# A fused attention and PEER block on one NeuronCore: both kv heads in one sliding unit, the key scores reloaded at other tiles, and other row counts in the searches and the tail

## The chip, the core and the metric

The kernel runs on one core of one Trainium2 chip. The metric is the device time of one execution in microseconds. TensorE is the matrix engine, VectorE the vector engine, ScalarE does activations and copies, GpSimd does some subtractions and issues gathers, SyncE issues most DMA transfers. In views of the profile they are PE (PEld for weight loads), DVE, ACT, POOL and SP.

## The reference

512 tokens of 1024 numbers go through a sliding-window attention with 8 heads on 2 kv heads, a latent attention with 8 heads, an output projection, and then a PEER layer: each token picks 16 of 16384 experts for each of 8 heads by two top-16 searches over 128 sub-keys and one over their sums, and adds up the picked experts.

```python
scores = jnp.einsum('bcqkgd,bcskd->bckgqs', qc, kb)            # sliding window: k = kv head, g = head in its group
scores = scores - slopes[None, None, :, :, None, None] * dist[:, :, None, None]
...
o = jnp.einsum('bckgqs,bcskd->bcqkgd', p / denom, vb)
x = x + gate1 * (jnp.concatenate([out_a, out_b], axis=-1) @ w_out)
...
s_top, i_top = lax.top_k(s, K)                                  # s: scores against the 2 x 128 sub-keys of a head
best, bi = lax.top_k(cand, K)                                   # cand: sums of the two lists of 16
a = jax.nn.gelu(jnp.einsum('tkd,td->tk', u_table[eb], xb), approximate=False)
y = jnp.einsum('tk,tkd->td', gb * a, v_table[eb])
```

## The kernel before

**Attention.** Work comes in units of one block of 128 queries. There are 16 sliding units (4 blocks, each with 2 kv heads and 2 pairs of query heads) and 32 latent units (4 blocks by 8 heads). For a sliding unit TensorE makes two score products in `scores` (L1028): both with the 64 rows of one kv head as contraction, so both use the same half of the array's rows, and both write one bank of PSUM, `u % 3`. VectorE adds the distance bias and takes the maximum (`bias_and_max`), ScalarE takes the exponentials, VectorE scales, TensorE transposes (L1041), ScalarE copies, TensorE multiplies by the values (L1058), VectorE copies out. In a step u TensorE issues `scores(u + 2)`, `transposes(u)`, `values(u - 1)`. `scores(u)` waits until the exponentials of unit u - 3 are done.

**The dense part of PEER.** 352 of the 512 tokens are computed against all 16384 experts: 128 tiles of the u table in a dot phase (`dot`, L1178 to L1180, 24 matmuls a tile), then 128 tiles of the v table in a mix phase (`mix`, L1229 to L1231). Each tile is loaded by SyncE into one of 3 buffers `raw`, rounded by ScalarE into `hi` (`high`), and its remainder is put into `lo` by GpSimd (`low_u`, L554), in the mix phase by VectorE (`low_v`). SyncE issues the load of tile m once the `lo` of tile m - 3 is done.

**The sparse part.** The other 160 tokens are computed from gathered expert rows. 128 of them have 128 row slots, the last 32 are spread over 4 partitions each and have 32 further slots: 160 u rows and 160 v rows in all, each a gather of 128 x 1024 numbers (512 KB), issued by GpSimd (`gather`, L567) into one of 7 buffers, four of which (`row_res`) lie where `res` was. Gather g waits until VectorE has used row g - 7. VectorE takes the dot product of a u row with the tokens (`row_dot`, L1549) and adds up a weighted v row (`row_sum`, L1684). A table `row_step` tells GpSimd after which tile each gather is issued, and the loops on VectorE have the matching counts.

**The searches.** `search(p)` for the four blocks of tokens runs on VectorE: `search(0)` first, and `search(1)` to `search(3)` during tiles 11 to 27, 44 to 60 and 77 to 93. Each reads the key scores from one tile `s`; for p of 1 to 3 SyncE reloads it from `keys` (L493, 1 MB) after it has waited for `s_free`, which VectorE raises when the first half of `search(p - 1)` is through with `s`. This load is at the tile `search_at[p - 1] + 10`, that is 10, 21 and 54. In a search VectorE makes a row dot at some of 15 pauses, `FILL[p]` in all. After each search come tiles in which TensorE also builds gates from one-hot matrices (28 to 43, 61 to 76, 94 to 105; L1189), with 2 or 3 row dots a tile. `turn_slots` (L1196) at the first of them waits for the end of the search.

**The tail.** In the tiles from 106 on (`tail_at`) there are no searches. VectorE does the 32 further row dots, planned at 3 a tile. At every sixth of them it also makes the `lo` of one tile (`own_low`: tiles 109, 111, 113, 115, 117, 119; L1694), so that GpSimd has a `lo` at every second tile and issues 6 gathers between. After the gelu of the dot products VectorE adds up 4 v rows (`EARLY`) ahead of the mix phase and the other 156 in it, 5 in every 4 tiles. After the last row sum SyncE reloads `res` from `x1` (L516, 2 MB), and VectorE makes the output from it (L1722).

## Time and profile before

| | us |
|---|---|
| median of 3 runs | 1495.96 |
| lowest and highest | 1495.47, 1498.05 |
| the profiled execution | 1498.4 |
| its span | 1496.6 |
| TensorE busy | 1419.4 (95%) |
| VectorE busy | 1207.9 (81%) |
| GpSimd busy | 744.9 (50%) |
| ScalarE busy | 708.8 (47%) |

Mean granted clock of TensorE: 0.967 of full speed. The span goes, in order of time, through the first projections (to 157 us), the attention (157 to 272), the output projection and the queries (to 384), the dot phase (384 to 1001), the mix phase (1001 to 1486) and the output. A busy TensorE is one that has a matmul under way, and does not tell at which clock. So the views to read are the waits of TensorE, the windows with the granted clock, and for each wait the order of time on the engine that it waits for.

### The profile page before, as it was taken

How to read it: one execution, taken by the hardware profiler on the slowest of the kernel's cores; microseconds unless marked ns; L12 is line 12 of the kernel's file. 1: busy time of each engine (PE TensorE's matmuls, PEld its weight loads, DVE VectorE, ACT ScalarE, POOL GpSimd, SP SyncE). 2: the span in 40 equal slices, each digit the busy share in tenths (PEclk: the TensorE clock that was granted, in tenths of full speed). 3: DMA queues.
4: the chain of work that ended last, by engine and by line, in shares of the span. 5: the costliest groups of instructions: out<-in, count | busy, mean ns of one | idle time of the engine just before them, and what ended most of it. 6: DMA issues, size and time to landing. Idle time of an engine off the chain costs nothing.

```text
span 1496.6 us, 23445 instructions
## 1 busy us (share of the span) xinstructions
PE 1419.4 (95%) x8415; PEld 1297.8 (87%) x8415; DVE 1207.9 (81%) x2637; ACT 708.8 (47%) x1315; POOL 744.9 (50%) x472
## 2 busy tenths in 40 slices
PE   3998999989998899999999998899999999999999
PEld 1464666768898899989999998899999999999998
DVE  4757567774878888958897876569999999999997
ACT  1245556331543588448854883243443434443342
POOL 2001000120577788768777876744555655565540
PEclk9999569999999999999999999899999999999999
DMA  9920100353678899999999999989999999999996
GB/s 330 328 84 1 56 1 1 119 205 127 211 248 286 314 340 338 360 389 319 328 348 402 335 325 359 404 263 373 397 388 389 382 401 392 398 390 389 394 386 229
DMA packets 158083, 438.79 MB, mean 293 GB/s; under 512 B 16592, under 2 KB 50704, under 8 KB 156816
## 3 DMA queue, kind: packets, MB, share of 16 engines
q1 hardware_dynamic: 91488, 244.55, 45.3%
q0 software_dynamic: 46080, 167.79, 29.4%
q10 hardware_dynamic: 20400, 24.95, 4.7%
q8 instruction: 67, 1.10, 0.3%
q14 instruction: 48, 0.39, 0.1%
HBM read 390.02 MB, written 47.22 MB: 292 GB/s over the span
## 4 chain that ended last, share of the span: by engine, by line
PE 83%; DMA 6%; DVE 4%; POOL 3%; ACT 2%; issue 1%; SPq 0%; ACTq 0%; DVEq 0%
PE ps L1230 11%; PE ps L1231 11%; PE ps L1229 11%; PE ps L1178 8%; PE ps L1180 8%; PE ps L1179 8%; PE ps L1189 5%; PE ps L947 4%; PE ps L1058 2%; POOL lo L554 2%; DMA raw<-in_u_tiles 2%; DMA row_res<-in_u_rows,E 2%; PE ps L1028 2%; PE ps L1041 2%; DMA ring<-in_w_ada 2%; PE ps L1031 1%
## 5 line engine op out<-in xcount | busy, mean ns | idle before, releaser
L804 ACT ACTIVATE hi<-raw 128x1024 fp32r<-128x1024 f32 x256 | 271.2, 1060 | 316.1 <-PE ps L1231 199.9
L554 POOL TENSOR_TENSOR lo<-raw,hi 128x1024 fp32r<-128x1024 f32 x122 | 293.3, 2408 | 156.0 <-ACT hi L804 155.3
L1178 PE MATMUL ps<-h2hi,hi 128*128 128x352 f32 x1024 | 339.6, 332 | 22.9 <-DVE lo L1694 11.6
L1180 PE MATMUL ps<-h2hi,lo 128*128 128x352 f32 x1024 | 334.6, 327 | 0.0
L1179 PE MATMUL ps<-h2lo,hi 128*128 128x352 f32 x1024 | 334.0, 326 | 0.0
L1230 PE MATMUL ps<-clo,hi 128*128 128x352 f32 x1008 | 324.2, 322 | 0.0
L1231 PE MATMUL ps<-chi,lo 128*128 128x352 f32 x1008 | 324.2, 322 | 0.0
L1229 PE MATMUL ps<-chi,hi 128*128 128x352 f32 x1008 | 324.1, 322 | 0.0
L567 POOL DMA_INDIRECT row_res<-in_v_tiles,E x91 | 153.0, 1681 | 134.9 <-DVE y_tok L1684 101.3
L1178 PEld LDWEIGHTS ps<-h2hi,hi 128*128 128x128 f32 x1024 | 196.8, 192 | 26.1 <-POOL lo L554 13.1
L1179 PEld LDWEIGHTS ps<-h2lo,hi 128*128 128x128 f32 x1024 | 195.8, 191 | 0.0
L1180 PEld LDWEIGHTS ps<-h2hi,lo 128*128 128x128 f32 x1024 | 195.4, 191 | 0.0
L1231 PEld LDWEIGHTS ps<-chi,lo 128*128 128x128 f32 x1008 | 189.3, 188 | 0.0
L1229 PEld LDWEIGHTS ps<-chi,hi 128*128 128x128 f32 x1008 | 189.3, 188 | 0.0
L1230 PEld LDWEIGHTS ps<-clo,hi 128*128 128x128 f32 x1008 | 189.3, 188 | 0.0
L1671 DVE TENSOR_TENSOR lo<-raw,hi 128x1024 fp32r<-128x1024 f32 x128 | 156.4, 1222 | 20.9 <-ACT hi L804 18.3
L567 POOL DMA_INDIRECT rows<-in_v_tiles,E x69 | 114.3, 1657 | 85.3 <-DVE y_tok L1684 67.7
L826 ACT ACTIVATE act_out<-ps 128x352 f32<-128x352 f32 x128 | 59.4, 464 | 140.6 <-PE ps L1180 127.7
L1549 DVE SCALAR_TENSOR_TENSOR row_res<-row_res,ps 128x1024 f32<-128x1024 f32 x91 | 108.7, 1216 | 12.0 <-DMA row_res<-in_u_rows,E 11.8
L837 ACT ACTIVATE ohW<-eqI,wS 128x128 f32<-128x128 f32 x352 | 107.4, 391 | 7.3 <-DVE eqI L1604 7.3
L567 POOL DMA_INDIRECT row_res<-in_u_rows,E x91 | 90.2, 991 | 30.8 <-issue 16.1
L1549 DVE SCALAR_TENSOR_TENSOR rows<-rows,ps 128x1024 f32<-128x1024 f32 x69 | 82.7, 1215 | 18.3 <-DMA rows<-in_u_rows,E 18.0
(293 smaller groups left out, 2202.8 us busy)
## 6 DMA issues: line engine op xcount, KB each, us to landing
raw<-in_u_tiles SPq DMA_DIRECT2D x128, 512.0 KB, 5.7
raw<-in_v_tiles SPq DMA_DIRECT2D x128, 512.0 KB, 7.2
gelus<-act_out ACTq DMA_DIRECT2D x128, 176.0 KB, 5.5
act_in<-gelus SPq DMA_DIRECT2D x128, 176.0 KB, 8.8
gates<-stage SPq DMA_DIRECT2D x32, 512.0 KB, 8.7
gate<-gates SPq DMA_DIRECT2D x32, 512.0 KB, 9.1
late<-in_w_ada SPq DMA_DIRECT2D x4, 2048.0 KB, 8.0
qkT<-in_w_ada SPq DMA_DIRECT2D x3, 2048.0 KB, 21.6
```

Of the source, the lines that this page charges most:

```text
L554: nc.gpsimd.tensor_tensor(lo[m % 3][:], raw[m % 3][:], hi[m % 3][:].bitcast(F32), ALU.subtract).then_inc(u_lo, 1)
L567: nc.gpsimd.indirect_dma_start(rows[g % NROWS], None, table, bass.IndirectOffsetOnAxis(ap=at, axis=0)).then_inc(row_in[g % NROWS], 16)
L804: nc.scalar.activation(hi[m % 3][:], raw[m % 3][:], ACT.Copy).then_inc(t_hi, 1)
L837: last = nc.scalar.activation(ohW[half][:, t, :], eqI[:, half, t, :], ACT.Copy, scale=wS[:, col:col + 1])
L1178: nc.tensor.matmul(out, hi[n % 3][:, cols], dense(h2hi, k), start=(k == 0), stop=False)
L1179: nc.tensor.matmul(out, hi[n % 3][:, cols], dense(h2lo, k), start=False, stop=False)
L1180: last = nc.tensor.matmul(out, lo[n % 3][:, cols], dense(h2hi, k), start=False, stop=(k == KD - 1))
L1229: nc.tensor.matmul(out, hi[m % 3][:, cols], chi[n % 4][:], start=(n == 0), stop=False)
L1230: nc.tensor.matmul(out, hi[m % 3][:, cols], clo[n % 4][:], start=False, stop=False)
L1231: last = nc.tensor.matmul(out, lo[m % 3][:, cols], chi[n % 4][:], start=False, stop=False)
L1549: nc.vector.scalar_tensor_tensor(out=row, in0=row, scalar=1.0, in1=x_tok, op0=ALU.mult, op1=ALU.mult, accum_out=aa[:, g:g + 1]).then_inc(r ...
L1671: tt_(lo[m % 3][:], raw[m % 3][:], hi[m % 3][:].bitcast(F32), ALU.subtract).then_inc(v_lo, 1)
```

## The change

Five things are changed.

1. A sliding unit is now one head g of both kv heads. Its two score products take rows 0 to 63 and rows 64 to 127, and write two banks of PSUM, (0, 1) or (2, 7) by turns. `scores(u)` for these waits for the bias of unit u - 2 and no longer for the exponentials; unit 0 also waits for the copy of a third block of queries. The rows of `w_out` are permuted on the host to match. The count and the shapes of all instructions stay.
2. The key scores are reloaded at tiles 6, 31 and 64.
3. The searches have 12, 10 and 10 row dots for 15, 9 and 9.
4. The tail has 2 row dots a tile for 3, GpSimd makes every `lo` of the dot phase, and the gelu of the row dots is at tile 125 (`more_at`), ahead of that tile's own gelu, for after tile 122.
5. No v row is added up ahead of the mix phase: all 160 are in it, still 5 in every 4 tiles, so that the last four come at its last three tiles.

```diff
-        units = [("s", b, kv, j) for b in range(TT) for kv in range(SKV) for j in (0, 2)] + \
+        units = [("s", b, None, g) for b in range(TT) for g in range(SG)] + \
                 [("m", b, h, 0) for b in range(TT) for h in range(MH)]
...
+        def score_bank(u, half):
+            return (0, 1, 2, 7)[2 * (u % 2) + half]
...
-        FILL, PAUSES, EARLY, MORE = {1: 15, 2: 9, 3: 9}, 15, 4, 4
+        FILL, PAUSES, MORE = {1: 12, 2: 10, 3: 10}, 15, 4
...
-        sums_at = [n for n in range(NT) for _ in range(2 if n % MORE == MORE - 1 else 1)][:SU - EARLY]
-        more_at = tail_at + 5 + (SU - SLOTS) // 3
-        row_step = row_step[:SLOTS] + [tail_at + 2 + j // 3 for j in range(SU - SLOTS)] + \
-            [more_at + 1 + j // 3 for j in range(EARLY)] + [NT + n for n in sums_at]
+        sums_at = [n for n in range(NT) for _ in range(2 if n % MORE == MORE - 1 else 1)][:SU]
+        more_at = tail_at + 3 + (SU - SLOTS) // 2
+        row_step = row_step[:SLOTS] + [tail_at + 2 + j // 2 for j in range(SU - SLOTS)] + [NT + n for n in sums_at]
...
-        own_low = [tail_at + 3 + 2 * j for j in range((SU - SLOTS) // 6 + 1)]
...
-                    if m == search_at[p - 1] + 10:
+                    if m == (6 if p == 1 else build_at[p - 1] + 3):
                         sp.wait_ge(s_free, p)
...
-                if m not in own_low:
-                    low_u(m)
+                low_u(m)
...
+                if n == more_at:
+                    act.wait_ge(row_used, SU)
+                    nc.scalar.activation(cc[:], aa[:], ACT.Gelu).then_inc(aa_gelu, 1)
                 if n >= NT - 3:
                     high_c(n - (NT - 3))
                 gelu(n)
...
-                if n == more_at + 1:
-                    act.wait_ge(row_used, SU)
-                    nc.scalar.activation(cc[:], aa[:], ACT.Gelu).then_inc(aa_gelu, 1)
...
                 if u == 0:
-                    pe.wait_ge(zq_sb, 2)
-                if u >= 3:
+                    pe.wait_ge(zq_sb, 3)
+                if 2 <= u < NSU + 3:
+                    pe.wait_ge(biased, min(u - 1, NSU))
+                if u >= NSU:
                     pe.wait_ge(exp_done, u - 2)
...
-                    rows = slice(sub * SD, (sub + 1) * SD)
-                    for j in range(2):
-                        c0 = j * 256 + (256 - len(tiles) * P)
-                        last = nc.tensor.matmul(ps[:, u % 3, c0:c0 + len(tiles) * P], qTs[rows, j0 + j, q], kcT[rows, 0, keys_],
+                    c0 = 512 - len(tiles) * P
+                    for half in range(2):
+                        rows = slice(half * SD, (half + 1) * SD)
+                        last = nc.tensor.matmul(ps[:, score_bank(u, half), c0:512], qTs[rows, j0, q], kcT[rows, 0, keys_],
                                                 start=True, stop=True)
...
             for g in range(SLOTS, SU):
-                if (g - SLOTS) % 6 == 0:
-                    m = own_low[(g - SLOTS) // 6]
-                    dve.wait_ge(t_hi, m + 1)
-                    tt_(lo[m % 3][:], raw[m % 3][:], hi[m % 3][:].bitcast(F32), ALU.subtract).then_inc(own_lo, 1)
                 row_dot(g)
...
-            for n in range(EARLY):
-                row_sum(n)
```

The diff shows a table entry where whole orders move, so the order of two queues stands here. First SyncE around tile 21. `raw` is a tile's load, `s<-keys` the reload that first waits for `s_free`. Before:

```order
L459 DMA raw_138<-in_u_tiles 128x1024
L493 DMA s<-keys 128x2048
L459 DMA raw_139<-in_u_tiles 128x1024
L459 DMA raw_140<-in_u_tiles 128x1024
L459 DMA raw_138<-in_u_tiles 128x1024
```

and now, at tile 31:

```order
L457 DMA raw_139<-in_u_tiles 128x1024
L491 DMA s<-keys 128x2048
L457 DMA raw_140<-in_u_tiles 128x1024
L457 DMA raw_138<-in_u_tiles 128x1024
L457 DMA raw_139<-in_u_tiles 128x1024
```

The reload stood behind the load of tile 21 and ahead of that of tile 22; it now stands ten tiles later.

Then GpSimd in the tail. `lo` is a tile's low part, `rows` and `row_res` are gathers. Before, around tile 114:

```order
L554 TENSOR_TENSOR lo_144<-raw_138,hi_141 128x1024
L567 DMA rows_149<-in_u_rows,E_133 128x1024
L567 DMA rows_150<-in_u_rows,E_133 128x1024
L567 DMA rows_151<-in_u_rows,E_133 128x1024
L567 DMA row_res_152<-in_u_rows,E_133 128x1024
L567 DMA row_res_153<-in_u_rows,E_133 128x1024
L567 DMA row_res_154<-in_u_rows,E_133 128x1024
L554 TENSOR_TENSOR lo_146<-raw_140,hi_143 128x1024
```

and now:

```order
L552 TENSOR_TENSOR lo_144<-raw_138,hi_141 128x1024
L565 DMA rows_151<-in_u_rows,E_133 128x1024
L565 DMA row_res_152<-in_u_rows,E_133 128x1024
L552 TENSOR_TENSOR lo_145<-raw_139,hi_142 128x1024
L565 DMA row_res_153<-in_u_rows,E_133 128x1024
L565 DMA row_res_154<-in_u_rows,E_133 128x1024
L552 TENSOR_TENSOR lo_146<-raw_140,hi_143 128x1024
```

Two low parts with six gathers between them (the low part of the tile between was on VectorE) have become a low part at every tile with two gathers after it. That pattern runs from tile 110 to 125.

## Rows read from the trace of the kernel before

**Rows 1.** Waits of PE, 384 to 1005 us: waiter, releaser, total us, times, longest.
```profile
PE ps L1178 <- DVE lo L1694: 11.6, 4, 4.6
PE ps L1178 <- POOL lo L554: 11.3, 5, 4.4
PE ps L1196 <- DVE IJW L1598: 7.1, 1, 7.1
```

**Rows 2.** Chain that ended last, in order of time: start, us, what.
```profile
202.53 2.00 PE ps L1028 x4
204.54 1.04 PE ps L1041 x4
205.58 1.06 PE ps L1058 x8
...
374.05 2.07 PE ps L1146 x32
```

**Rows 3.** Windows: stretch, busy us of each engine, PEclk, DMA share, GB/s.
```profile
184.00:192.00 8.00, 8.00 (x33) 5.15 (x32) 4.82 (x16) 3.28 (x10) 0.00 (x0) 0.50 0.00 1
...
770.00:825.00 55.00, 55.00 (x343) 54.84 (x342) 45.87 (x173) 23.47 (x31) 40.83 (x23) 1.00 1.02 389
...
956.00:964.00 8.00, 4.28 (x15) 4.28 (x15) 4.65 (x7) 1.17 (x2) 5.96 (x4) 0.66 1.03 415
```

**Rows 4.** Timeline of a sliding unit: start, us, engine line op [idle before <-releaser].
```profile
188.15 0.75 DVE L1435 SCALAR_TENSOR_TENSOR pb<-distm,ps 128x256 f32<-128x256 f32 x2 [1.63 <-PE ps L1028]
```

**Rows 5.** Timeline, tiles 19 to 22: low part, loads, first matmul of tile 22.
```profile
454.42 2.40 POOL L554 TENSOR_TENSOR lo<-raw,hi 128x1024 fp32r<-128x1024 f32 x1 [0.35 <-ACT hi L804]
...
463.59 0.33 SPq L493 DMA_DIRECT2D s<-keys  x1
463.96 15.86 SPq L459 DMA_DIRECT2D raw<-in_u_tiles  x5
...
476.02 0.66 PE L1178 MATMUL ps<-h2hi,hi 128*128 128x352 f32 x1 [4.37 <-POOL lo L554]
```

**Rows 6.** Timeline of search(1): start, two row dots, an index search, turn_slots after it.
```profile
431.79 3.18 DVE L1529 MAX8 sv<-s 128x8 f32<-128x128 f32 x16
443.21 1.22 DVE L1549 SCALAR_TENSOR_TENSOR rows<-rows,ps 128x1024 f32<-128x1024 f32 x1 [8.24 <-DMA rows<-in_u_rows,E]
...
448.09 0.28 DVE L1532 FIND_INDEX8 six<-sv,s 128x8 uint32<-128x128 f32 x1
...
482.01 1.22 DVE L1549 SCALAR_TENSOR_TENSOR rows<-rows,ps 128x1024 f32<-128x1024 f32 x1 [4.82 <-DMA rows<-in_u_rows,E]
...
508.72 0.90 PE L1196 MATMUL ps<-ident,IJW 128*128 128x128 f32 x3 [7.11 <-DVE IJW L1598]
```

**Rows 7.** Chain in order of time at tile 55, and its first matmul (timeline).
```profile
629.06 13.60 DMA raw<-in_u_tiles
...
646.25 0.43 PE L1178 MATMUL ps<-h2hi,hi 128*128 128x352 f32 x1 [3.19 <-POOL lo L554]
```

**Rows 8.** Timeline: a GpSimd set (low part, second gather), first matmuls of tiles 112, 127.
```profile
879.92 2.40 POOL L554 TENSOR_TENSOR lo<-raw,hi 128x1024 fp32r<-128x1024 f32 x1
...
883.75 0.94 POOL L567 DMA_INDIRECT row_res<-in_u_rows,E  x1 [0.30 <-issue]
...
918.68 0.33 PE L1178 MATMUL ps<-h2hi,hi 128*128 128x352 f32 x1
...
997.29 0.32 PE L1178 MATMUL ps<-h2hi,hi 128*128 128x352 f32 x1
```

**Rows 9.** Timeline of the end: a row sum, reload of res, output.
```profile
1475.01 1.28 DVE L1684 SCALAR_TENSOR_TENSOR y_more<-row_res,cc,y_more 128x1024 f32<-128x1024 f32 x1
...
1479.60 0.33 SPq L516 DMA_DIRECT2D res<-x  x1
...
1487.24 4.05 DVE L1722 SCALAR_TENSOR_TENSOR res<-ps,ada,res 128x512 f32<-128x512 f32 x6 [5.91 <-DMA res<-x]
...
1493.04 0.75 DVE L1722 SCALAR_TENSOR_TENSOR res<-ps,ada,res 128x512 f32<-128x512 f32 x1 [0.55 <-PE ps L1250]
```

More of the change, by code:

```diff
@@ L292, in build @@
         u_lo = sem("u_lo")
-        own_lo = sem("own_lo")
         v_lo = sem("v_lo")
@@ L398, in build @@
         assert len(row_step) >= SLOTS
-        sums_at = [n for n in range(NT) for _ in range(2 if n % MORE == MORE - 1 else 1)][:SU - EARLY]
-        more_at = tail_at + 5 + (SU - SLOTS) // 3
-        row_step = row_step[:SLOTS] + [tail_at + 2 + j // 3 for j in range(SU - SLOTS)] + \
-            [more_at + 1 + j // 3 for j in range(EARLY)] + [NT + n for n in sums_at]
+        sums_at = [n for n in range(NT) for _ in range(2 if n % MORE == MORE - 1 else 1)][:SU]
+        more_at = tail_at + 3 + (SU - SLOTS) // 2
+        row_step = row_step[:SLOTS] + [tail_at + 2 + j // 2 for j in range(SU - SLOTS)] + [NT + n for n in sums_at]
         assert len(row_step) == 2 * SU
-        own_low = [tail_at + 3 + 2 * j for j in range((SU - SLOTS) // 6 + 1)]
-        def low_done(m):
-            mine = sum(o <= m for o in own_low)
-            return (own_lo, mine) if m in own_low else (u_lo, m + 1 - mine)
         x_tok = ps[:, 4:6, :].rearrange("p a c -> p (a c)")
@@ L454, in load_tile @@
                 if 3 <= m < NT + 3:
-                    sp.wait_ge(*low_done(m - 3))
+                    sp.wait_ge(u_lo, m - 2)
                 elif m >= NT + 3:
@@ L1053, in values @@
                     if kind == "s":
-                        v = z[:, kb, Z_V + sub * SD:Z_V + (sub + 1) * SD]
+                        v = z[:, kb, Z_V + half * SD:Z_V + (half + 1) * SD]
                     else:
@@ L1172, in dot @@
             def dot(n):
-                pe.wait_ge(*low_done(n))
+                pe.wait_ge(u_lo, n + 1)
                 pe.wait_ge(gelu_done, n + 1)
@@ L1460, in copy_out @@
                 if kind == "s":
-                    ins = nc.vector.tensor_copy(oT[:, 2 * sub + j0 // 2, cols], ps[:, 3 * (u % 2) + 3, 0:P])
+                    ins = nc.vector.tensor_copy(oT[:, j0, cols], ps[:, 3 * (u % 2) + 3, 0:P])
                 else:
@@ L1715, in _ @@
                     if at == n:
-                        row_sum(EARLY + j)
+                        row_sum(j)
                 if n + 3 < NT:
@@ L1748 @@
         "mla_norms": np.stack([a["mla_q_norm"][0], a["mla_k_norm"][0]], 1),
-        "w_out": a["w_out"][0], "peer_w_query": a["peer_w_query"][0],
+        "w_out": np.concatenate([a["w_out"][0][:SH * SD].reshape(SKV, SG, SD, D).transpose(1, 0, 2, 3).reshape(SH * SD, D),
+                                 a["w_out"][0][SH * SD:]]), "peer_w_query": a["peer_w_query"][0],
         "sub_keys": a["peer_sub_keys"][0].transpose(1, 3, 0, 2).reshape(P, PH, NK),
```

7 lines of the change are left out of this document (4 added, 3 removed).

## The prediction

> **What bounds the kernel now.** I read the waits of TensorE first, then windows for the granted clock, then for each wait the timeline of the engine it waits for. In the dot phase TensorE is the bound wherever it is not stopped: 343 matmuls in 55.0 us, 0.160 us each, so 24 of them, one tile, take 3.85 us [rows 3]. It is stopped by three kinds of waits, 30 us in all: 11.6 for low parts on VectorE, 11.3 for low parts on GpSimd, 7.1 for the end of search(1) [rows 1]. In the sliding units of the attention it is never idle, 8.00 of 8 us, but at half the clock [rows 3], and a unit is the plain sum of its three pieces: 2.00 for scores, 1.04 for transposes, 1.06 for values [rows 2]. VectorE waits 1.63 us a unit for the scores [rows 4]. In the mix phase TensorE is busy without a gap. So what counts is what TensorE does in the units, and when each low part and the end of search(1) come.
>
> **Paired kv heads.** Nothing is added; the two products of a unit change from the same array rows to different ones. The nearest row is that of the key scores, the same form (64 rows in turn from either half, different banks): 16 products of 128 columns in 2.07 us at full clock [rows 2]. The unpaired 256 columns take 1.00 us each at half clock, which is 0.25 for 128 columns at full clock, so 16 would take 4.0: pairs take 0.52 of that. A unit's scores then take 1.04 instead of 2.00. Bounds: no overlap at all, gain 0; complete overlap, gain 1.00. I take 0.96, since the row is of this very form. Twelve units have 256 columns: 12 x 0.96 = 11.5 us. The four with 128 columns lie beside VectorE's work at the start; I count nothing (0 to 1). What is late next: TensorE's unit shrinks from 4.10 to 3.14, VectorE is busy 4.82 of 8 us, 2.47 a unit [rows 3], so TensorE stays the bound, with 0.6 to spare. The new wait for the bias of two units back was met long before, and the wait for a third block of queries holds TensorE only where it turned heads anyway. **-11.5**, between -9.5 and -13.
>
> **The reload at tile 21 and search(1).** The low part of tile 19 is done at 454.42 + 2.40 = 456.8, which frees the load of tile 22. It goes at 463.96, right behind the reload at 463.59, which waited for search(1) to let go of `s` [rows 5]. Seven microseconds late, it makes TensorE wait 4.37 us. At tile 31 search(1) is over and nothing waits. What is late next is search(1) itself: TensorE waits for its end at the first gate tile until 508.72, for 7.11 us [rows 6]. Without the first stall tile 22 starts at 476.02 - 4.37 = 471.65 and tile 28 is reached six tiles later, at 494.75. Does VectorE get there by then? It starts at 431.79 and needs 76.6 us until 508.4. Of this 8.24 and 4.82 are waits for rows [rows 6]. The second came because GpSimd's gather stood behind the late low part; it goes. Of the first, 4.0 us go: with 12 rows the first pause has none, and the 16 index searches after it (444.4 to 448.4 [rows 6]) now stand ahead of the first row. Three row dots of 1.2 us go to later places: 3.5. Together 76.6 - 4.8 - 4.0 - 3.5 = 64.3: the search ends at 496.1, or somewhat before if later rows are waited for less too. That is 0 to 1.3 behind tile 28. TensorE's gain is 508.7 - 495.4 = 13.3, and some 0.7 of slower clock after the stall. **-14**, between -10 and -15. The reload at tile 6 meets `s_free` within 1 us of it, with buffers to spare: 0.
>
> **Searches 2 and 3.** The reload at tile 54 puts 1 MB into a stretch that is full: the load of tile 55 took 13.60 us and TensorE waited 3.19 [rows 7]. Search(3) has the same gates and no reload, and there TensorE is busy 55.0 of 55 us at 389 GB/s [rows 3]. So the 3.2 go. Each search gets one more gather, 0.52 MB, 1.35 us at that rate, somewhere between hidden and paid in full. The reloads at 31 and 64 lie in gate tiles, which last longer for much the same traffic; their 2.7 us of transfer are covered by three `raw` and seven row buffers. **-2.5**, between 0 and -3.5.
>
> **The tail.** Tile 112 starts at 918.68 and tile 127 at 997.29 [rows 8]: 78.6 us for 15 tiles that take 57.8, so 20.8 are lost, to the four waits for VectorE's low parts (which stood behind row dots that waited for gathers), to one of 2.3 us for GpSimd's low part, and to the clock that fell with them, to 0.66 in one stretch [rows 3]. Now GpSimd has every low part and two gathers a tile. One such set takes 884.69 - 879.92 = 4.77 us [rows 8], against 3.85 for TensorE: GpSimd becomes the bound, by 0.92 a tile. It runs from tile 110 to 125, 15 steps, 13.8 us. Its lead takes some of this away: three buffers let it start two tiles, 7.7 us, ahead, less its own 2.40 and ScalarE's rounding; I take 3 (0 to 5). So 11 to 12 are lost where 20.8 were. **-9**, between -2 and -13. Transfers: 0.52 MB for the tile, 1.05 for two rows, 0.18 for gelus are 1.75 MB, 4.2 us at the 415 GB/s that the tail reached [rows 3], below 4.77. The Trainium skill has less ("SBUF — State Buffer", section "A bandwidth-pool intuition that's wrong"): about 358 GB/s between HBM and a core. By that a tile would take 4.9 us, and by an estimate from it the tail would gain 2 us less; the rows with 389 and 415 GB/s speak against it.
> The gelu of the row dots at tile 125 waits for the last row dot, whose gather goes at tile 122; what is queued behind it on ScalarE is that tile's gelu, for which tile 127 waits. I see a microsecond of room and count 0 (0 to 2).
>
> **The end.** Before, the reload of `res` goes at 1479.60, lands at 1487.2, and VectorE has been idle since 1481.33 [rows 9]. The last row sums now come after tile 127's low parts: 1481.3 plus four of 1.28 is 1486.4. The reload takes the same 7.6 us, to 1494.0, and now VectorE's eight output steps of 0.675 (4.05 for six) all lie behind it: 1499.4, where the last ended at 1493.79. **+5.6**, between +5 and +7: the cover for this reload was TensorE's last two tiles, and it is gone.
>
> **Sum.** -11.5 - 14 - 2.5 - 9 + 5.6 = -31.4. The profiled execution took 1498.4 (span 1496.6), 2.4 above the median; the difference is taken from the median: 1495.96 - 31.4 = 1464.6.
>
> **Rivals.**
> A, *the clock comes up in the sliding units*. Row pairs keep more of the array at work. The rows only say that a busy TensorE stays at 0.50 there [rows 3]. At 2.4 GHz its unit would be 1.57 us and VectorE's 2.47, with some 0.1 of handover, would bound: 3.14 - 2.6 = 0.54 less, 12 times, 6.5 us: 1458. The Trainium skill ("TensorE: Matmul & The Clock Gate", Part 1) has activity release the clock; by that alone the stage would have been at full clock before, and the row disagrees. Its Part 4 says that transposes don't count as activity, which would fit. Chance 0.15.
> B, *the tail gives nothing*. GpSimd's sets stretch or loads come late, as in the 415 GB/s stretch, and 20.8 are lost again: 1464.6 + 9 = 1474. Against it: the rate asked for is 367 GB/s at 4.77 us a tile. Chance 0.16.
> C, *the pairs don't overlap*, the change doesn't do what it says: 1464.6 + 11.5 = 1476. Against it the key scores' row. Chance 0.07.
> D, *slower*: TensorE, with a gap in each tile of the tail, is granted half the clock there. A tile would take 7.7 instead of 4.77: 2.9 for 15 tiles, 44 us, 1508. It decides from 11 such tiles on. For it: 0.66 in a stretch with waits [rows 3]. Against: that had a wait of 4.6 us [rows 1], here they are 0.9. Chance 0.04.
>
> **How the numbers follow.** The forecast has 0.58, its own range 1459 to 1472 from the bounds above, not all at one end. The range must take in most of A and B: 1456 to 1476, which leaves out D, half of C and the outer ends of the others. Only D is slower by over 0.2%, and nothing but a mixture of B, C and a worse end lands within 0.2% (about what can be told from no change): faster 0.95, same 0.01, slower 0.04.
>
> **What would show it.** Scores of a unit in about 1.04 in the chain, and the granted clock there; no wait of the reload at its new tiles; `turn_slots` waiting under 2 us and reached near 495 less the attention's gain; no 3 us wait in search(2); low part and two gathers each 4.8 us in the tail, with waits of TensorE under 1 us; the reload of `res` 7 us later against the last tiles, and eight output steps in a row. Wrong it would be if the tail's loads are late, or if search(1) ends several microseconds after tile 27.

## The result, and the profile after

| | before | after |
|---|---|---|
| median, us | 1496.62 (1495.47 to 1498.05, 4 runs) | 1463.50 (1462.56 to 1464.45, 4 runs) |
| profiled execution: time, span, mean granted clock | 1498.4, 1496.6, 0.967 | 1464.15, 1462.3, 0.986 |
| first dot (tile 0) | 384.16 | 364.83 |
| tile 112, tile 127 | 918.68, 997.29 | 886.40, 956.24 |

The changed kernel takes 0.9778 of the time before (95% interval 0.9761 to 0.9795), 33.1 us less. The forecast was 1464.6, with a range of 1456 to 1476. The total is right. Two of its five terms are not: they miss by 7.8 and 5.6 us, in opposite directions.

To see that, the two traces are laid beside each other by the starts of the tiles. Each term of the sum has its edit between two such marks, and the marks of the two kernels can be subtracted. What a stretch takes also depends a little on where it starts: pair_alone below shows 2 to 3 us of that in stretches whose code is unchanged.

| stretch | term | before, us | after, us | difference | predicted |
|---|---|---|---|---|---|
| start to tile 0 | paired heads | 384.16 | 364.83 | -19.3 | -11.5 |
| tile 0 to tile 29 | reload, search(1) | 131.74 | 123.39 | -8.4 | -14 |
| tile 29 to tile 112 | searches 2 and 3 | 402.78 | 398.18 | -4.6 | -2.5 |
| tile 112 to tile 127 | tail | 78.61 | 69.84 | -8.8 | -9 |
| tile 127 to the end of the span | end | 499.31 | 506.06 | +6.8 | +5.6 |
| sum | | | | -34.3 | -31.4 |

**The page of the changed kernel.** TensorE's busy time, the granted clock in 40 slices, and the shares of the chain that ended last by engine:

```profile
PE 1390.9 (95%) x8415; PEld 1274.4 (87%) x8415; DVE 1200.6 (82%) x2631; ACT 710.3 (49%) x1315; POOL 772.1 (53%) x478
...
PEclk9999799999999999999999999999999999999999
...
PE 80%; DVE 7%; POOL 4%; DMA 4%; ACT 2%; issue 1%; SPq 1%; ACTq 0%; DVEq 0%; POOLq 0%
```

The clock row has one low digit, the fifth (146 to 183 us), in which the sliding units begin.

**The waits of TensorE** in the changed kernel, from the first dot to the end (waiter, releaser, total us, times, longest); they answer to [rows 1]:

```profile
PE ps L1177 <- POOL lo L552: 9.6, 14, 1.1
PE ps L1195 <- DVE IJW L1597: 4.4, 1, 4.4
PE ps L1248 <- DVE y_more L1683: 3.2, 1, 3.2
```

Waits for VectorE's low parts are gone, since VectorE has none left. GpSimd's are many and short where they were few and long: the tail has a bound now, and no stalls (the 1.1 is at tile 3; in the tail none is over 0.7). The wait for search(1) fell from 7.1 to 4.4 where 0 to 1.3 was predicted. The last row is new, and belongs to the end.

**The sliding units.** Windows of the changed kernel, TensorE alone (stretch, its length, busy us, PEclk, DMA share, GB/s), and one with all engines (PE, PEld, DVE, ACT, POOL); they answer to the first window of [rows 3]:

```profile
160.00:170.00 10.00, 9.34 (x44) 0.55 0.32 119
172.00:174.00 2.00, 2.00 (x13) 0.50 0.00 0
174.00:176.00 2.00, 2.00 (x18) 0.85 0.00 0
176.00:178.00 2.00, 1.55 (x18) 1.00 0.00 0
...
180.00:188.00 8.00, 6.50 (x60) 3.88 (x56) 7.72 (x28) 5.59 (x17) 0.00 (x0) 1.00 0.01 3
```

In the full units the granted clock is first at the lower of its two levels, as before, and at the higher one, 2.4 GHz, from 176 us on. What the engine did before it rose: from 162 us on it was busy without a gap, with pairs, transposes and values. Before, it was as busy, with single score products, and the clock stayed at 0.50 up to 214. While the clock is at 0.50, the chain that ended last has the score products of a unit (start, us, what; two products, each in two records) as

```profile
164.70 1.16 PE ps L1027 x4
```

where the kernel before has 2.00 [rows 2]. From 176 us on VectorE is the busiest engine (7.72 of 8 us) and TensorE waits for it: one unit follows the other in 2.38 us.

**Search(1).** Its first step on VectorE starts at 412.39, and `turn_slots` gets its result at 479.83. Timeline, [idle before <-releaser], and windows behind this wait, here and (the last line) behind the 7.11 us wait of the kernel before:

```profile
479.83 0.90 PE L1195 MATMUL ps<-ident,IJW 128*128 128x128 f32 x3 [4.38 <-DVE IJW L1597]
...
480.40:485.00 4.60, 4.60 (x18) 4.60 (x17) 4.23 (x8) 2.45 (x8) 3.79 (x4) 0.50 1.03 417
485.00:488.00 3.00, 3.00 (x24) 3.00 (x23) 1.13 (x3) 0.80 (x2) 1.76 (x2) 0.97 1.03 416
...
509.00:514.00 5.00, 5.00 (x26) 5.00 (x26) 4.34 (x8) 2.45 (x8) 4.52 (x4) 0.75 1.03 408
```

The clock is at 0.50 until about 485.2, 5.3 us behind the wait. Before, with the longer wait, it was at 0.50 for only 2.8 us behind it (0.75 in the mean of the 5 us shown).

**The tail.** GpSimd's queue, timeline, as in [rows 8]:

```profile
878.08 2.41 POOL L552 TENSOR_TENSOR lo<-raw,hi 128x1024 fp32r<-128x1024 f32 x1
880.65 0.96 POOL L565 DMA_INDIRECT row_res<-in_u_rows,E  x1 [0.16 <-issue]
881.91 0.94 POOL L565 DMA_INDIRECT row_res<-in_u_rows,E  x1 [0.30 <-issue]
882.87 2.43 POOL L552 TENSOR_TENSOR lo<-raw,hi 128x1024 fp32r<-128x1024 f32 x1
```

One set takes 882.87 - 878.08 = 4.79 us (predicted 4.77), and from tile 114 to 125 each tile takes 4.77 to 4.79.

**The end.** Timelines of SyncE's queue and of VectorE; they answer to [rows 9]:

```profile
1443.27 2.70 DVE L1683 SCALAR_TENSOR_TENSOR y_more<-row_res,cc,y_more 128x1024 f32<-128x1024 f32 x2
...
1445.99 0.33 SPq L514 DMA_DIRECT2D res<-x  x1
...
1454.01 5.36 DVE L1715 SCALAR_TENSOR_TENSOR res<-ps,ada,res 128x512 f32<-128x512 f32 x8 [8.04 <-DMA res<-x]
```

The last row sum ends at 1445.97, the reload goes 0.02 us later, and all eight output steps lie behind its landing, 5.36 us in a row.

### The profile page after: what moved, and what is told of

Same layout as the page of the kernel before. It is cut to its first block, busy times and chain, and to the rows that moved or that the text cites. A ratio compares the mean times of both kernels' runs of the same rounds, so it can differ in the third digit from the quotient of the medians.

```text
span 1462.3 us, 23449 instructions
## 1 busy us (share of the span) xinstructions
PE 1390.9 (95%) x8415; PEld 1274.4 (87%) x8415; DVE 1200.6 (82%) x2631; ACT 710.3 (49%) x1315; POOL 772.1 (53%) x478
## 4 chain that ended last, share of the span: by engine, by line
PE 80%; DVE 7%; POOL 4%; DMA 4%; ACT 2%; issue 1%; SPq 1%; ACTq 0%; DVEq 0%; POOLq 0%
PE ps L1228 11%; PE ps L1229 11%; PE ps L1230 11%; PE ps L1177 8%; PE ps L1179 8%; PE ps L1178 8%; PE ps L1188 5%; PE ps L944 5%; POOL lo L552 3%; PE ps L1057 2%; DMA qkc<-in_w_ada 2%; PE ps L1030 1%; DMA rows<-in_u_rows,E 1%; POOL row_res L565 1%; PE ps L1098 1%
## 5 line engine op out<-in xcount | busy, mean ns | idle before, releaser
L552 POOL TENSOR_TENSOR lo<-raw,hi 128x1024 fp32r<-128x1024 f32 x128 | 307.9, 2408 | 143.7 <-ACT hi L801 142.9
L565 POOL DMA_INDIRECT row_res<-in_v_tiles,E x91 | 159.0, 1748 | 119.7 <-DVE y_tok L1683 80.8
L565 POOL DMA_INDIRECT rows<-in_v_tiles,E x69 | 122.0, 1769 | 84.5 <-DVE y_tok L1683 67.2
```

The source lines that it names most:

```text
L552: nc.gpsimd.tensor_tensor(lo[m % 3][:], raw[m % 3][:], hi[m % 3][:].bitcast(F32), ALU.subtract).then_inc(u_lo, 1)
L565: nc.gpsimd.indirect_dma_start(rows[g % NROWS], None, table, bass.IndirectOffsetOnAxis(ap=at, axis=0)).then_inc(row_in[g % NROWS], 16)
```

## The experiments

The kernels ran in three groups of four (the first four rows of the table, the next four, the last four), each group on one chip beside the kernel before. Groups differ by more than a small edit does: the median of the kernel before was 1500.5 in the first two and 1497.4 in the third. The ratios are to the kernel before of the same group; where one microsecond matters, the distances between tiles of a trace decide, since they hang less on what came ahead.

| run | median, us | lowest to highest | ratio to before (95%) |
|---|---|---|---|
| pair_alone | 1476.81 | 1474.95 to 1484.13 | 0.9868 (0.9827 to 0.9909) |
| same_rows | 1484.07 | 1482.07 to 1485.39 | 0.9906 (0.9876 to 0.9935) |
| same_rows_filler | 1496.20 | 1492.27 to 1509.35 | 0.9985 (0.9961 to 1.0009) |
| psum_operands | 1461.11 | 1460.49 to 1461.75 | 0.9749 (0.9720 to 0.9778) |
| reload_old | 1468.73 | 1463.77 to 1470.46 | 0.9781 (0.9733 to 0.9829) |
| fill_old | 1471.99 | 1470.30 to 1472.56 | 0.9797 (0.9748 to 0.9845) |
| tail_old | 1464.15 | 1461.96 to 1465.03 | 0.9742 (0.9693 to 0.9790) |
| end_parts | 1459.46 | 1458.12 to 1461.89 | 0.9712 (0.9664 to 0.9761) |
| after_again | 1462.91 | 1460.61 to 1464.03 | 0.9760 (0.9737 to 0.9782) |
| own_3rd | 1456.30 | 1453.97 to 1458.54 | 0.9722 (0.9699 to 0.9745) |
| all_but_tail | 1456.34 | 1455.58 to 1458.31 | 0.9724 (0.9702 to 0.9745) |
| all_three | 1450.93 | 1448.04 to 1453.74 | 0.9689 (0.9667 to 0.9711) |

### What brings the clock up in the sliding units

**pair_alone**: the kernel before with the paired units, and nothing else of the change. Its core, from the change's diff:

```diff
-        units = [("s", b, kv, j) for b in range(TT) for kv in range(SKV) for j in (0, 2)] + \
+        units = [("s", b, None, g) for b in range(TT) for g in range(SG)] + \
```

> The kernel before with the paired units alone (reloads, rows in the searches, tail and end as before). The two traces put the first dot 19.3 us earlier (384.16 to 364.83), where the sum had 11.5. Theory: the pairs give all of it, since TensorE's clock comes up inside the sliding units (first at about 174 us, 1.00 from 176 on in the trace of the changed kernel, 0.50 throughout before): first dot within 1 us of 364.8, and the time 17 to 20 us below the kernel before, 1477 to 1479. Rival 1: the clock came up by chance in that one execution: 11 to 12 us below, 1484 to 1485. Rival 2: the earlier start moves search(1) against the low parts and gives part of it back: first dot at 364.8 and the time only 10 to 15 us below.

Measured: first dot at 361.92, 22.2 us earlier than in the kernel before, and 2.9 earlier than expected; the median 1476.81 is 20 us under the 1496.6 of the result's table, and 23.7 under the kernel before of its own group. So the pairs alone give the whole gain of the attention, clock included. Rival 2 has a point: search(1) ends later in this kernel (below), which takes 3.5 of the 22.2 back. But stretches further on, with the code of the kernel before, are shorter than there: tiles 29 to 112 take 400.6 us instead of 402.8 (the wait at tile 55 is 1.1 us instead of 3.2, with the reload still at tile 54), and tiles 112 to 127 take 76.0 instead of 78.6. The window over eight microseconds of its sliding units:

```profile
170.00:178.00 8.00, 6.50 (x59) 1.00 0.00 1
```

**same_rows**: the changed kernel with both products on one half of the array.

```diff
-                        rows = slice(half * SD, (half + 1) * SD)
+                        rows = slice(0, SD)
```

> The changed kernel, both score products of a sliding unit from the first 64 array rows (so the second half has the scores of the first kv head's rows instead of its own): order, banks and waits stay, only the pairing in the array goes. Theory: a unit's scores take 2.00 us again at granted clock 0.50, which stays there through all sliding units, the unit 4.1 us; the first dot comes 18 to 20 us later than 364.8, the time 17 to 20 us above the changed kernel. Rival: the new order, banks or heads in a unit brought the clock up and not the pairing: the clock comes up all the same, scores 1.0 us at full clock, unit 2.4 to 2.7 us, and the time is under 5 us above.

Measured: 20.6 us above the changed kernel (in another group), first dot at 382.61. TensorE is never idle in its sliding units, one unit follows the other in 4.1 us, and the clock stays down until 212.6, about when they end:

```profile
160.00:180.00 20.00, 20.00 (x68) 0.50 0.18 66
180.00:200.00 20.00, 20.00 (x79) 0.50 0.01 2
```

The order of the heads, the four banks and the new wait have no part in it; only the place in the array differs.

**same_rows_filler**: a full-height product ahead of each pair.

```diff
+                        if half == 0:
+                            nc.tensor.matmul(ps[:, score_bank(u, 0), 384:512], qTs[:, j0, q], kcT[:, 0, q],
+                                             start=True, stop=True)
```

> As same_rows (both score products from the first 64 rows, second half not its own scores), with one product more in each sliding unit, 128 columns over all 128 array rows, whose result is overwritten by the unit's first product. It adds 0.25 us a unit at full clock, 0.50 at half. Theory: what holds the clock at 0.50 is that a unit's products use half the rows; with the filler it comes up within the first units, the unit is then 1.00 + 0.25 + 0.52 + 0.53 = 2.3 us of TensorE at full clock, under VectorE's 2.4, and the kernel is 10 us or more faster than same_rows although it does more, within 8 us of the changed kernel. Rival: the clock stays at 0.50; the unit takes 4.6 us and the kernel is 6 to 8 us slower than same_rows.

Measured: slower than same_rows by 12 us, twice what the rival said, first dot at 394.37, and the clock at 0.50 all the way:

```profile
160.00:180.00 20.00, 18.77 (x59) 0.50 0.25 94
180.00:200.00 20.00, 20.00 (x76) 0.50 0.00 0
200.00:215.00 15.00, 15.00 (x59) 0.50 0.01 2
```

The added product takes 0.73 us of a unit of 4.83, not the 0.50 expected, in the chain that ended last:

```profile
191.58 0.73 PE ps L1028 x2
192.31 2.00 PE ps L1030 x4
194.31 1.04 PE ps L1043 x4
195.36 1.06 PE ps L1060 x8
```

My theory fell. One product over all 128 rows in each unit, 0.73 of its 4.83 us, does not bring the clock up. Two at a time in separate halves do, in all eleven profiled executions of a kernel with pairs, somewhere between 167.9 and 174.6 us. What in the pairs does it, the two at once or the shorter unit, was not told apart.

### What sets the end of search(1)

The trace of the changed kernel shows three short VectorE instructions of search(1) that take far longer than their twins. Timelines of VectorE and of GpSimd around them:

```profile
438.89 2.40 POOL L552 TENSOR_TENSOR lo<-raw,hi 128x1024 fp32r<-128x1024 f32 x1 [0.35 <-ACT hi L801]
439.80 1.64 DVE L1564 CAST sixf<-six 128x256 f32<-128x256 uint32 x1
...
458.23 2.40 POOL L552 TENSOR_TENSOR lo<-raw,hi 128x1024 fp32r<-128x1024 f32 x1 [0.36 <-ACT hi L801]
458.26 2.51 DVE L1578 SCALAR_TENSOR_TENSOR bia<-qr 128x128 f32<-128x128 f32 x1
460.81 0.30 DVE L1580 TENSOR_TENSOR ps<-qr,bia 128x128 f32<-128x128 f32 x1
...
477.25 2.36 POOL L552 TENSOR_TENSOR lo<-raw,hi 128x1024 fp32r<-128x1024 f32 x1
478.38 1.39 DVE L1597 TENSOR_TENSOR IJW<-eW,eR 128x128 f32<-128x128 f32 x1
```

Each starts while a low part of GpSimd runs and ends 0.14 to 0.16 us after it: 441.44 against 441.29, 460.77 against 460.63, 479.77 against 479.61. Outside a low part they take 0.28 to 0.30. The row dots, which have one operand in PSUM, take 1.2 us whether a low part runs or not.

**psum_operands**: an operand of the second and of the third moved to PSUM.

```diff
-                settled(nc.vector.tensor_copy(qr[:], bia[:]))
+                nc.vector.tensor_copy(qr0, bia[:, 0, :, :])
+                settled(nc.vector.tensor_copy(qr[:, 1, :, :], bia[:, 1, :, :]))
...
-                settled(nc.vector.scalar_tensor_tensor(out=bia[:, 0, :, :].bitcast(F32), in0=qr[:, 0, :, :], scalar=float(half),
+                settled(nc.vector.scalar_tensor_tensor(out=bia[:, 0, :, :].bitcast(F32), in0=qr0, scalar=float(half),
...
-                settled(nc.vector.reciprocal(eR[:], eS[:]))
+                settled(nc.vector.reciprocal(eR, eS[:]))
```

(`qr0` and `eR` are columns of bank 1 of PSUM now.)

> The changed kernel; in the searches two intermediate values (the row part of the cast indices and the reciprocal of the sums) are written to PSUM instead of SBUF, so that the two VectorE instructions that took 2.51 us instead of 0.29 and 1.39 instead of 0.29 in search(1) read one operand from PSUM. Theory: they were held by GpSimd's low part running at the same time (458.23 to 460.63, 477.25 to 479.61), because both their operands lay in SBUF; now they take 0.3 to 0.4 each, search(1) ends 3 us sooner, TensorE's wait at tile 28 falls from 4.4 to about 1.2 us, and the time falls by 3 to 4.5 us, with the clock staying up at tile 28. Rival 1: they are held whatever their operands: same durations, same time. Rival 2: the end of search(1) hangs on something else on VectorE: they get short and the wait stays at 4 us.

Measured, the same places in its timeline:

```profile
456.97 2.41 POOL L554 TENSOR_TENSOR lo<-raw,hi 128x1024 fp32r<-128x1024 f32 x1 [0.34 <-ACT hi L803]
457.15 0.29 DVE L1581 SCALAR_TENSOR_TENSOR bia<-ps,qr 128x128 f32<-128x128 f32 x1
457.48 0.30 DVE L1583 TENSOR_TENSOR ps<-ps,bia 128x128 f32<-128x128 f32 x1
457.69 1.85 DVE L1584 TENSOR_TENSOR ps<-qr,bia 128x128 f32<-128x128 f32 x1
...
475.92 2.38 POOL L554 TENSOR_TENSOR lo<-raw,hi 128x1024 fp32r<-128x1024 f32 x1
476.66 0.28 DVE L1600 TENSOR_TENSOR IJW<-eW,ps 128x128 f32<-128x128 f32 x1
```

The two instructions take 0.29 and 0.28 us in the midst of a low part. The next one that still has both operands in SBUF is held in their place, until 459.54, 0.16 behind the low part's end. So it is the operands. That one took half of the gain back: the wait at tile 28 fell from 4.4 to 2.9, not to 1.2, and the time by 1.8 to 2.4 us, not 3 to 4.5. The Trainium skill ("SBUF — State Buffer", section "Who interferes with whom") has this rule: a VectorE instruction with two SBUF inputs and a GpSimd instruction that reads SBUF exclude each other, and a cast can too; the trace agrees, 2.51 against 0.29 us. The rule spoke against part of this change's gain, and the prediction did not weigh it.

**reload_old** and **fill_old** take the two edits on search(1) apart.

```diff
-                    if m == (6 if p == 1 else build_at[p - 1] + 3):
+                    if m == (6 if p == 1 else search_at[p - 1] + 10):
```

> The changed kernel with the reloads of the key scores for searches 2 and 3 back at their old tiles (21 and 54); rows, tail and pairing stay. Theory of the prediction: the reload at tile 21 stands ahead of a tile load until search(1) lets go of the scores, TensorE waits some 4 us at tile 22, one of GpSimd's gathers stands behind the late low part and search(1) ends 4 to 5 us later; the wait at tile 28 stays about 4 us since both move together, and a 3 us wait comes back at tile 54 or 55. Time 7 to 9 us above the changed kernel. Rival: the stall at tile 22 only takes room from the wait at tile 28, since the end of search(1) is set by VectorE alone: the wait at tile 28 shrinks to 0 to 1 us and the time is 3 to 4 us above, from searches 2 and 3.

```diff
-        FILL, PAUSES, MORE = {1: 12, 2: 10, 3: 10}, 15, 4
+        FILL, PAUSES, MORE = {1: 15, 2: 9, 3: 9}, 15, 4
```

> The changed kernel with 15, 9 and 9 rows in the searches instead of 12, 10 and 10. Theory: search(1) has three row dots of 1.2 us more and waits for the first row ahead of the 16 index searches, 3.6 and 4 us, so TensorE's wait for it rises from 4.4 to 11 or 12 us and the time by 6 to 8 us. Rival: what set the end of search(1) in the changed kernel was the three VectorE instructions that GpSimd's low parts held (4.7 us in sum); with other rows these fall elsewhere, and the rise is only 2 to 4 us.

Measured, with pair_alone as the fourth corner; us from tile 0 to the first dot of tile 28 in the profiled executions:

| | 15, 9, 9 rows | 12, 10, 10 rows |
|---|---|---|
| reload at tile 21 | 128.6 (pair_alone) | 116.4 (reload_old) |
| reload at tile 31 | 122.4 (fill_old) | 115.6 (after_again 115.7) |

The rows alone give 12.2 of the 13.0 us, the reload alone 6.2. With the 125.1 us of the kernel before in that corner it is 8.7 and 2.7, of 9.5. Either way they don't add up, because each alone takes away the stall at tile 22: neither reload_old nor fill_old waits there. In reload_old, with three row dots less, and with the first index searches ahead of the first row instead of behind a wait for it, search(1) lets go of the scores sooner, the reload at tile 21 goes 5.7 us sooner (73.83 us after tile 0 against 79.55 in pair_alone), and the load behind it is in time. Its tiles 21 and 22 take 7.73 us together, no stall; the theory's 4 us did not come, and the wait at tile 28 is 5.2 us. It has 0.8 us more at tile 28 and 2.0 more between tiles 54 and 61 (29.4 against 27.4), where 3 were expected. Its profiled execution took 1463.8 and the three others 1468.6 to 1470.5; what these spent 5 us on no trace shows. fill_old went about as the theory has it: TensorE's wait rose to 10.9 us, the time by 8 to 9 where 6 to 8 were expected.

The first row of this table also corrects the base of the sum. The kernel before had 125.1 us there, pair_alone has 128.6 with the same code in the searches. Its search(1) took 80.1 us instead of 76.9. Of the 3.3 us, 2.4 are its last instruction, which met a low part, and 1.1 a longer wait for a row; in search(1) of the kernel before no such instruction was held for more than 0.25 us. Timeline of pair_alone:

```profile
487.21 2.67 DVE L1605 TENSOR_TENSOR IJW<-eW,eR 128x128 f32<-128x128 f32 x1
...
487.37 2.35 POOL L559 TENSOR_TENSOR lo<-raw,hi 128x1024 fp32r<-128x1024 f32 x1
```

Here the trace has the VectorE instruction start 0.16 us ahead of the low part, while GpSimd issues a gather, and it is held to the low part's end all the same. Whether the gather's issue has a part in it was not told apart.

### The tail and the end

**tail_old**: the tail and the early row sums of the kernel before in the changed one.

```diff
-        row_step = row_step[:SLOTS] + [tail_at + 2 + j // 2 for j in range(SU - SLOTS)] + [NT + n for n in sums_at]
+        row_step = row_step[:SLOTS] + [tail_at + 2 + j // 3 for j in range(SU - SLOTS)] + \
+            [more_at + 1 + j // 3 for j in range(EARLY)] + [NT + n for n in sums_at]
+        own_low = [tail_at + 3 + 2 * j for j in range((SU - SLOTS) // 6 + 1)]
```

> The changed kernel with the tail of the kernel before: three rows a tile, six low parts of the tail on VectorE, the first four row sums ahead of the mix. From the traces the new tail saved 8.8 us between tile 112 and tile 127 and cost 6.8 at the end, so of the two only 2 are left. Theory: the time is 1 to 3 us above the changed kernel; tiles 112 to 127 take 78 us instead of 70, and the reload of the residual goes before TensorE's last tiles, with the output 6 to 7 us nearer to them. Rival: the new tail gives its full 9 us and the late end has another cause (the queue, the last row sums by themselves): 8 to 9 us above.

Measured: 1464.15, within 1.3 us of the changed kernel's two medians. Tiles 112 to 127 take 78.0 us instead of 69.8, and from tile 127 to the end of the span 499.5 instead of 506.1. So the fourth and fifth parts of the change moved time from one place to another: 8.2 us in the tail against 6.6 at the end, and nothing that the medians can show.

**end_parts** keeps the tail and mends the end.

```diff
+        def place_of(g):
+            return rows[(g + 5) % NROWS]
...
-            sp.wait_ge(row_used, 2 * SU)
-            sp.dma_start(res[:], x1).then_inc(x1_in, 16)
+            for j in range(4):
+                sp.wait_ge(row_used, 2 * SU - 6 + j)
+                sp.dma_start(res[:, 2 * j:2 * j + 2, :], x1[:, 2 * j:2 * j + 2, :]).then_inc(x1_in[j], 16)
...
-                if d == 0:
-                    pe.wait_ge(row_used, 2 * SU)
-                    pe.wait_ge(spread_ready, 1)
+            pe.wait_ge(row_used, 2 * SU)
+            pe.wait_ge(spread_ready, 1)
+            for d in range(KD):
+                cols = slice(d * P, (d + 1) * P)
                 nc.tensor.transpose(ps[:, d, ND * P:T], y_tok[:, cols], ident[:])
```

> The changed kernel with another end: the rows rotate through their buffers so that the last three lie outside the residual's place, the residual is reloaded in four parts as each place comes free, and TensorE does the last tiles' products ahead of the transposes that need the row sums. Theory: the reload behind the last row sum is what sets the end (it went at 1445.99 and landed 8.0 us later, and TensorE waited 3.2 us for the sums): the last part now goes 3 to 4 us earlier and is a quarter as long, the output steps start on time, and the time falls by 4 to 7 us. Rival: the parts land no sooner, because the queues are full of the last gathers: under 2 us.

Measured: 1459.46, 3.5 to 4 us under the changed kernel's medians, at the lower end of the theory or just short of it. The output steps no longer wait for the reload. But they wait for TensorE, and all eight still come in a row:

```profile
1451.48 5.36 DVE L1720 SCALAR_TENSOR_TENSOR res<-ps,ada,res 128x512 f32<-128x512 f32 x8 [3.92 <-PE ps L1254]
```

My edit had put all transposes behind all products, so the first output was as late as the last.

**own_3rd**: what bounds a tile of the tail.

```diff
+        own_low = [tail_at + 4 + 3 * j for j in range(5)]
...
             for g in range(SLOTS, SU):
+                if (g - SLOTS) % 6 == 0 and (g - SLOTS) // 6 < len(own_low):
+                    m = own_low[(g - SLOTS) // 6]
+                    dve.wait_ge(t_hi, m + 1)
+                    tt_(lo[m % 3][:], raw[m % 3][:], hi[m % 3][:].bitcast(F32), ALU.subtract).then_inc(own_lo, 1)
                 row_dot(g)
```

> The changed kernel, every third low part of the tail on VectorE (five of them), two rows a tile as before. Theory of the prediction: a tile of the tail takes 4.77 us because GpSimd's set of one low part and two gathers takes that long; with a third of the low parts off it, three tiles take 2 x 4.77 + 2.4 = 11.9 us and TensorE's 3.85 nearly bounds; tiles 112 to 127 take 60 to 62 us instead of 70 and the time falls by 7 to 9 us. Rival: the transfers bound close behind. A tile brings 1.75 MB, and the tail ran at 358 GB/s with the DMA engines 0.98 busy; then a tile still takes 4.5 us or more, and the time falls by 3 us at most. Second rival: VectorE's low parts stand behind row dots that wait for gathers, TensorE waits 2 to 4 us for each as in the tail before, and nothing is gained.

Measured: 6.6 us under after_again; tiles 112 to 127 take 63.9 us, 4.26 a tile. Windows over the same stretch of the tail in after and own_3rd (busy us of PE, PEld, DVE, ACT, POOL, then PEclk, DMA share, GB/s):

```profile
890.00:940.00 50.00, 43.44 (x256) 40.51 (x255) 24.82 (x42) 16.32 (x22) 44.69 (x33) 1.00 0.99 371
```

```profile
890.00:940.00 50.00, 47.07 (x282) 44.74 (x280) 35.58 (x47) 18.15 (x24) 44.28 (x31) 1.00 1.03 412
```

GpSimd was the bound, as predicted, but not for its full 0.92 us a tile. The prediction put the traffic of a tile at 4.2 us by the 415 GB/s of [rows 3]; the tail now runs at 412 GB/s and 4.26 us a tile, beside five tiles that still take 4.8 (three of them, 123 to 125, lie behind the last low part on VectorE). It lies between theory and first rival; the second is out, TensorE waits for no low part of VectorE.

**after_again** is the changed kernel once more, for comparison with the three others of its group.

> The changed kernel itself, once more, beside the next three on one chip: 1463.5 within 3 us, first dot between 361.9 and 364.8 (the spread of the paired kernels so far).

Measured 1462.91, first dot at 363.31.

**all_but_tail**: psum_operands with the flag in PSUM too, other rows, and end_parts with the transposes from the fourth output on.

```diff
-        FILL, PAUSES, MORE = {1: 12, 2: 10, 3: 10}, 15, 4
+        FILL, PAUSES, MORE = {1: 10, 2: 11, 3: 11}, 15, 4
...
+                settled(nc.vector.scalar_tensor_tensor(out=odd, in0=qr0, scalar=float(half),
...
+                tt_(abf[:, 0, :, :], qr[:, 0, :, :], odd, ALU.add)
+                settled(tt_(abf[:, 1, :, :], qr[:, 1, :, :], odd, ALU.subtract))
...
+                if d < KD // 2 - 1:
+                    continue
+                if d == KD // 2 - 1:
                     pe.wait_ge(row_used, 2 * SU)
                     pe.wait_ge(spread_ready, 1)
+                for e in range(KD // 2) if d == KD // 2 - 1 else (d,):
```

> The changed kernel with three edits: all three VectorE instructions of a search's index part with one operand in PSUM (the one that took the hold over in psum_operands, 1.85 us, too), 10, 11 and 11 rows in the searches, and the end in parts with the row sums' transposes from the fourth output on. Theory: TensorE's wait at tile 28 goes (4.4 us, of which holds are 3.3 and two row dots 2.4) with 1 to 2 us of half clock behind it, and the output steps start 4 us sooner than in end_parts: 4.5 to 6 us from the search and 5 to 7 from the end, 1451 to 1454. Rival 1: the rows moved to searches 2 and 3 cost what they save, 1.3 us each on full queues: 1454 to 1457. Rival 2: the end is bound by the row sums themselves and gives only the 2 to 3 us that end_parts gave: 1455 to 1458.

Measured: 6.6 us under after_again, where the theory had 9 to 12. Two of three parts did what they were to. The wait at tile 28 is 0.6 us, the clock stays at 1.00 behind it, and tile 29 comes 117.1 us after tile 0 instead of 123.3. The output steps follow TensorE again:

```profile
1444.55 4.20 DVE L1727 SCALAR_TENSOR_TENSOR res<-ps,ada,res 128x512 f32<-128x512 f32 x6 [0.64 <-PE ps L1260]
```

The third part, the rows, cost 7 us: from tile 29 to 112 it takes 405.7 us instead of 398.6. With 11 rows in searches 2 and 3 a gather comes up for issue before its buffer is free. Timelines of GpSimd and TensorE in search(3):

```profile
743.79 1.90 POOL L572 DMA_INDIRECT rows<-in_u_rows,E  x1 [4.91 <-DVE rows L1559]
745.71 2.37 POOL L559 TENSOR_TENSOR lo<-raw,hi 128x1024 fp32r<-128x1024 f32 x1
...
748.13 0.66 PE L1184 MATMUL ps<-h2hi,hi 128*128 128x352 f32 x1 [2.23 <-POOL lo L559]
```

GpSimd stands 4.91 us for a row dot, the low part behind it is late, and TensorE waits 2.23 us, behind which its matmuls take 0.50 us instead of 0.32. That is 4.1 us at tiles 82 and 83. The same wait of 2.23 us in search(2) costs 2.4 at tile 49, and there the clock stays at 1.00; tile 60 has 0.8 more. This is rival 1 with another mechanism: not the queues' traffic, but the order in GpSimd's own queue.

**all_three**: all_but_tail with the edit of own_3rd.

> all_but_tail with every third low part of the tail on VectorE as in own_3rd. Theory: the gains add, so the difference from all_but_tail is that of own_3rd from the changed kernel within 2 us. Rival: with the tail shorter, the row sums start the mix with their buffers less far ahead and the end comes no sooner: under half of own_3rd's gain.

Measured: 5.4 us under all_but_tail, where own_3rd gave 6.6: the gains add. It takes 0.9689 of the time of the kernel before, and beats the changed kernel by 12 us.

## Why the prediction was right in total, and where it was not

The total is right in part by luck: the first term missed by 7.8 us one way and the second by 5.6 the other.

**Paired heads, -11.5, measured -19.3. The step that failed is the clock.** The overlap was right: in the chain the score products of a unit take 1.16 us at half clock, where 1.04 was said and 2.00 stood before. But the sum took 0.50 as given for the whole stage, from a row of unpaired units, and gave the other case 0.15. It was the case that came. Its price was well worked out: VectorE at 2.57 us a unit was to bound, 2.38 is what it takes, and 18.0 instead of 19.3 us was the estimate. same_rows and pair_alone show from either side that the pairs do it.

**Reload and search(1), -14, measured -8.4.** **The step that failed is the length of search(1).** TensorE was at the gate where the sum had it (110.6 us after tile 0, predicted 110.6), and search(1) started where it was said. It took 67.4 us instead of 64.3. Three instructions were held by low parts (1.34, 1.97 and 1.10 us over the durations in the trace of before, 4.4 together), and against that the third wait for a row, 1.57, went as well. The remaining 0.3 is a misreading: 508.4, which the sum took as the end of the search before, is the start of its last instruction, and its end is 508.66. Another 2 us are the clock: I had 0.7 of slower clock saved, and the trace has 5.3 us at 0.50 behind the wait at tile 28, where the kernel before had 2.8. The last 0.6 was in the sum itself, which set TensorE's start between tile 28 and the end of the search, and not at that end. The **attribution** failed too: I gave the stall at tile 22 and the second wait for a row to the reload's place. fill_old shows that this place does remove them, but reload_old shows that the rows alone do as well.

**Searches 2 and 3, -2.5, measured -4.6.** The 3.2 us wait at tile 55 went, and the additional gathers cost nothing: tiles 61 to 93 take 151.7 us, 152.2 before. But 2.2 of the 4.6 are there in pair_alone too, which has neither edit. Against pair_alone the two edits give 2.4, and reload_old, which takes the reload back, is 2.0 to 2.4 us longer in this stretch. So -2.5 was right for what the edits do. One more each is one too many (all_but_tail).

**Tail, -9, measured -8.8.** Right by its own steps: the set of 4.77 (4.79), the bound on GpSimd, twelve tiles that pay it, waits of 0.7 us at most, and no loss of clock. Its arithmetic has a slip: 13.8 less a lead of 3 is 10.8, and the sum went on with 11 to 12; measured are 12.1 us lost (69.8 less 57.8), so the lead was worth 1.7 us. That 20.8 were lost before is also in part chance, since pair_alone lost 18.2 with the same code. The gelu at tile 125 cost nothing.

**End, +5.6, measured +6.8.** Right in mechanism: reload behind the last row sum, then eight steps in a row. The reload went 7.4 us later against tile 127 instead of 6.8 and landed in 8.0 instead of 7.6. Together with the tail it was worth 2.0 us between the two traces, and nothing that the medians show (tail_old); the prediction had 3.4 us for the two.

**Bandwidth.** The estimate by the Trainium skill's 358 GB/s ("SBUF — State Buffer", section "A bandwidth-pool intuition that's wrong") was rightly left aside: 50 us of the tail ran at 371 GB/s in the changed kernel and at 412 with GpSimd relieved.

## What to carry to other kernels

Sum a change between fixed marks of the program, and let the marks tell afterwards: a right total may hide two wrong terms. When two edits are aimed at one stall, price them together and each alone, since the second often finds it gone. Before a chain of short VectorE instructions is given its length from a trace, look which of them read two operands from SBUF while GpSimd works there: what they took in one schedule hangs on where the low parts fall. Here one operand in PSUM took the hold away from the two instructions that got it, and the next one with both operands in SBUF was held in their place.

## What the runs showed of the hardware

- TensorE's granted clock stayed at 0.50 for 54.6 us of work on single 64-row products, transposes and values (before, same_rows), and for 64.9 us with a full-height product in each unit (same_rows_filler). With the score products in pairs it rose to 1.00 after 10 to 17 us at 0.50, in eleven of eleven profiled executions.
- A VectorE instruction of 0.29 us takes up to 2.94 us (reload_old) when it meets a GpSimd low part and has both operands in SBUF, and casts from SBUF to SBUF are held too (1.64 instead of 0.30). With one operand in PSUM the two that were moved take 0.29 and 0.28 us inside a low part (psum_operands).
- The hold can last over two low parts in a row: among the first weights for the mix phase in the kernel before, an instruction with both operands in SBUF, 0.53 us elsewhere, takes 5.75 us (at 988.55; low parts of 4.74 us from 989.17 on).
- After a wait of 4.4 us at tile 28 TensorE ran at 0.50 for 5.3 us, which cost about 2 us more. After 7.1 us in the kernel before it was 2.8 us; after 0.6 us (all_but_tail) it stayed at 1.00; after 2.2 us (all_but_tail again) it stayed at 1.00 once and fell once. So the length of the wait alone doesn't tell the cost.
- The core drew 412 GB/s over 50 us of the tail of own_3rd.
